# mLSTM queries and keys turned by VectorE's 32x32 squares and transfers through memory, with their copies and convolutions two and three units later

## What is computed

```python
qk, v, o, gates, z = jnp.split(x @ w_in, [o1, o2, o3, o4], axis=-1)   # qk: 8 heads x 128 queries, then keys
qk = jax.nn.silu(_causal_depthwise_conv(qk, conv_w, conv_b))          # 4 taps along the sequence
q, k = jnp.split(qk, 2, axis=-1)
# per head: s_qk = q k^T * exp(gates), then s_qk v, norm, output gates
```

## Time and profile before

| | us |
|---|---|
| median of 3 runs | 1828.47 (1828.24 to 1828.49) |
| the profiled execution, its own time | 1828.43 |
| span of the profiled execution | 1826.6 |
| PE busy | 1813.7 (99% of the span) |
| DVE busy | 1267.3 (69%) |
| ACT busy | 942.7 (52%) |

### The profile page before, as it was taken

How to read it: one execution, slowest core, us unless ns; L and a number is a source line. 1 busy time by engine, 2 the same in 40 slices (tenths; PEclk the granted TensorE clock), 3 DMA queues, 4 the chain that set the end, 5 groups by cost and what they waited for, 6 DMA issues and landing times.

```text
span 1826.6 us, 24598 instructions
## 1 busy us (share of the span) xinstructions
PE 1813.7 (99%) x8999; PEld 1531.1 (84%) x8999; DVE 1267.3 (69%) x1711; ACT 942.7 (52%) x1310; POOL 38.0 (2%) x116
## 2 busy tenths in 40 slices
PE   8999999999999999999999999999999999999999
PEld 7899998888888888887888888888888888888887
DVE  6676766588556755767887878787767556577764
ACT  4545554455465555636554545555435444565542
POOL 2000000000000004000000000000000000000000
PEclk9999999999999999999999999999999999999999
DMA  8565454668889887575555555544547776555453
GB/s 293 162 177 148 139 175 156 202 179 185 177 153 212 175 179 176 191 238 159 174 175 152 167 173 154 179 154 160 185 138 232 217 217 209 162 160 163 159 166 113
DMA packets 172909, 323.61 MB, mean 177 GB/s; under 512 B 16584, under 2 KB 23136, under 8 KB 172048
## 3 DMA queue, kind: packets, MB, share of 16 engines
q1 hardware_dynamic: 171680, 317.89, 60.6%
q10 hardware_dynamic: 576, 4.19, 0.6%
q0 software_dynamic: 560, 0.26, 0.1%
HBM read 318.11 MB, written 4.19 MB: 176 GB/s over the span
## 4 chain that ended last, share of the span: by engine, by line
PE 98%; DVE 1%; ACT 0%; DMA 0%; issue 0%; DVEq 0%
PE acc L366 28%; PE acc L368 28%; PE acc L367 27%; PE ps L615 2%; PE ps L2760 2%; PE ps L463 1%; PE acc L332 1%; PE acc L333 1%; PE acc L331 1%; PE ps L648 1%; PE acc L350 0%; PE acc L349 0%; PE acc L353 0%; PE acc L355 0%; PE acc L348 0%; PE acc L354 0%
## 5 line engine op out<-in xcount | busy, mean ns | idle before, releaser
L299 DVE TENSOR_TENSOR wlo<-wraw,whi 128x1024 fp32r<-128x1024 f32 x579 | 699.1, 1222 | 337.4 <-ACT whi L284 334.4
L284 ACT ACTIVATE whi<-wraw 128x1024 fp32r<-128x1024 f32 x579 | 599.9, 1052 | 365.8 <-PE acc L368 333.4
L366 PE MATMUL acc<-whi,ta_hi 128*128 128x512 f32 x1664 | 659.7, 396 | 3.6 <-DVE ta_lo L548 2.0
L368 PE MATMUL acc<-whi,ta_lo 128*128 128x512 f32 x1664 | 649.2, 390 | 0.0
L367 PE MATMUL acc<-wlo,ta_hi 128*128 128x512 f32 x1664 | 647.8, 389 | 0.0
L366 PEld LDWEIGHTS acc<-whi,ta_hi 128*128 128x128 f32 x1664 | 312.6, 188 | 68.7 <-DVE ta_lo L548 3.4
L368 PEld LDWEIGHTS acc<-whi,ta_lo 128*128 128x128 f32 x1664 | 312.3, 188 | 66.9
L367 PEld LDWEIGHTS acc<-wlo,ta_hi 128*128 128x128 f32 x1664 | 312.8, 188 | 62.1
L366 PE MATMUL acc<-whi,tb_hi 128*128 128x512 f32 x576 | 228.4, 396 | 0.0
L368 PE MATMUL acc<-whi,tb_lo 128*128 128x512 f32 x576 | 224.9, 390 | 0.0
L367 PE MATMUL acc<-wlo,tb_hi 128*128 128x512 f32 x576 | 224.4, 390 | 0.0
(11 more groups left out here) (325 smaller groups left out, 1644.8 us busy)
## 6 DMA issues: line engine op xcount, KB each, us to landing
wraw<-in_ml_w_in SPq DMA_DIRECT2D x129, 512.0 KB, 5.8
wraw<-in_a_w_in SPq DMA_DIRECT2D x128, 512.0 KB, 3.9
wraw<-in_kv_w SPq DMA_DIRECT2D x64, 512.0 KB, 4.0
wraw<-in_b_w_in SPq DMA_DIRECT2D x64, 512.0 KB, 4.4
wraw<-in_mla_w_in SPq DMA_DIRECT2D x49, 512.0 KB, 4.6
wraw<-in_mla_w_out SPq DMA_DIRECT2D x32, 512.0 KB, 3.8
wraw<-in_ml_w_out SPq DMA_DIRECT2D x32, 512.0 KB, 4.4
wraw<-in_a_w_out SPq DMA_DIRECT2D x32, 512.0 KB, 3.8
```

The source lines that it names most:

```text
L284: nc.scalar.activation(unit_of(whi, n, SPLIT, w), unit_of(wraw, n, RAW, w), ACT.Copy).then_inc(w_high, 1)
L299: nc.vector.tensor_tensor(unit_of(wlo, n, SPLIT, w), unit_of(wraw, n, RAW, w), unit_of(whi, n, SPLIT, w).bitcast(F32), ALU.subtract).then_ ...
L366: nc.tensor.matmul(o, xh, wh, start=first, stop=False)
L368: m = nc.tensor.matmul(o, xl, wh, start=False, stop=end)
```

## The change

The eight PE transposes per tile go away, for queries and keys of both halves. In their place DVE turns 32x32 squares of the evacuated tile into `cin` (`qk_square`, two instructions), right after it has copied the tile out of PSUM: DVE's unit 9 and 18 in the first half, 10 and 18 in the second (`QK_EVAC`; for s = 0 it counts places in the phase, 1 and 10). SP writes `cin` to memory after its load 8 places later, and reads it back into `qkw1` with four transfers after its load 10 places later (`turn_qk`). ACT's `window_in` copies from `qkw1` into `cin`, now two instructions of 128x512 from SBUF. `L1_AT` moves: queries from 11 to 13, keys from 19 to 22, and with them `window_in`, `conv`, `conv_sigmoid` and `conv_gate`; `weigh` stays after unit 27.

```diff
-        L1_AT = {"q": 11, "k": 19, "ws": [27, 33, 39, 45], "nm": [31, 37, 43, 49], "g0": 56, "t0": 60}
+        L1_AT = {"q": 13, "k": 22, "ws": [27, 33, 39, 45], "nm": [31, 37, 43, 49], "g0": 56, "t0": 60}
+        QK_EVAC = {(0, 0): 1, (0, 1): 10, (1, 0): 10, (1, 1): 18}
+        def qk_squares_of(v):
+            return cin[:, :, PAD:].rearrange("p j (b h c) -> p b j h c", b=TB, h=4)[:, v]
...
+            def turn_qk(name, p):
+                for (s, j), at in QK_EVAC.items():
+                    n = 2 * s + j
+                    if name == f"l1_{s}" and p == at + 8:
+                        sp.wait_ge(l1["q_sq"], TB * (n + 1))
+                        sp.dma_start(qk_squares.rearrange("p (j r) -> p j r", j=4), cin[:, :, PAD:]).then_inc(l1["q_out"], 16)
+                    if name == f"l1_{s}" and p == at + 10:
+                        sp.wait_ge(l1["q_out"], 16 * (n + 1))
+                        for i in range(4):
+                            rows = qkw1[32 * i:32 * i + 32, 1024 * j:1024 * j + 1024]
+                            sp.dma_start(rows.rearrange("q (i r) -> q i r", i=4),
+                                         qk_squares.rearrange("(i q) (j r) -> j q i r", i=4, j=4)[i]).then_inc(l1["q_in"], 16)
...
             def window_in(s, j):
                 n = 2 * s + j
-                act.wait_ge(l1["q_pe"], n + 1)
-                if n > 0:
-                    act.wait_ge(l1["y_ok"], 4 * n)
+                act.wait_ge(l1["q_in"], 64 * (n + 1))
                 act.wait_ge(l1["pads"], 2)
-                nc.scalar.activation(cin[:, :, PAD:], ps2(0).rearrange("p (h t) -> p h t", t=T),
-                                     ACT.Copy).then_inc(l1["q_c"], 1)
+                y = qkw1[:, 1024 * j:1024 * j + 1024].rearrange("p (i b h c) -> p b h i c", i=4, b=TB, h=4)
+                for b in range(TB):
+                    nc.scalar.activation(cin[:, :, PAD + b * P:PAD + (b + 1) * P].rearrange("p h (i c) -> p h i c", i=4),
+                                         y[:, b], ACT.Copy).then_inc(l1["q_c"], 1)
...
+            def qk_square(s, j):
+                landed(dve, *l1_at(s, j))
+                if 2 * s + j > 0:
+                    dve.wait_ge(l1["y_ok"], 4 * (2 * s + j))
+                for b in range(TB):
+                    v = qkw[j][:, b, :].rearrange("p (h j c) -> p j h c", h=4, j=4)
+                    nc.vector.transpose(qk_squares_of(b), v).then_inc(l1["q_sq"], 1)
...
-            def window(s, j):
-                landed(pe, *l1_at(s, j))
-                pe.wait_ge(tr_lo, turn.n)
-                if 2 * s + j > 0:
-                    pe.wait_ge(l1["q_c"], 2 * s + j)
-                if s > 0:
-                    pe.wait_ge(l1["st"], 4 * s)
-                for h in range(4):
-                    for b in range(TB):
-                        m = nc.tensor.transpose(ps2(0)[:, h * T + b * P:h * T + (b + 1) * P],
-                                                qkw[j][:, b, h * P:(h + 1) * P], ident[:])
-                m.then_inc(l1["q_pe"], 1)
...
             def weigh(s, c):
                 h = c % 4
                 pe.wait_ge(l1["q_r"], 2 * s + 2)
-                pe.wait_ge(l1["q_c"], 2 * s + 2)
+                if h == 0:
+                    pe.wait_ge(tr_lo, turn.n)
...
-                for j in range(2):
-                    if u == L1_AT["qk"[j]]:
-                        window(s, j)
```

More of the change, by code:

```diff
@@ L112, in build @@
         ARENA = 14016
+        qk_squares = nc.dram_tensor("qk_squares", (P, 2 * COLS), F32).ap()
         arena = sb("arena", [P, ARENA])
@@ L794, in build @@
         L1_GATES = ("l1_g", 1)
-        l1 = sems(1, "g_in g_pe g_row g_e g_m g_pe2 g_col q_pe q_c y_ok y_e q_r sc arg ex sel st nm "
+        QK_EVAC = {(0, 0): 1, (0, 1): 10, (1, 0): 10, (1, 1): 18}
+        def qk_squares_of(v):
+            return cin[:, :, PAD:].rearrange("p j (b h c) -> p b j h c", b=TB, h=4)[:, v]
+        l1 = sems(1, "g_in g_pe g_row g_e g_m g_pe2 g_col q_sq q_out q_in q_c y_ok y_e q_r sc arg ex sel st nm "
                      "den h ssq var rs og ge z_ok pads")
@@ L1051, in _ @@
                         load(name, p)
+                        turn_qk(name, p)
                 else:
@@ L2011, in gates_c @@
                 nc.vector.tensor_copy(acol, ps[:, 3, 0:16].rearrange("p (b h) -> p b h", b=TB)).then_inc(l1["g_col"], 1)
+            def qk_square(s, j):
[5 more added lines that the diff above has]
+                    nc.vector.transpose(qk_squares_of(b), v).then_inc(l1["q_sq"], 1)
             def conv(s, j, heads):
                 n = 2 * s + j
-                dve.wait_ge(l1["q_c"], n + 1)
+                dve.wait_ge(l1["q_c"], TB * (n + 1))
                 if s > 0:
@@ L2096, in l1_side @@
                 u = p if s else p + 8
+                for j in range(2):
+                    if p == QK_EVAC[(s, j)]:
+                        qk_square(s, j)
                 if s == 0 and p == 4:
```

## The result

| | before | after |
|---|---|---|
| median, us | 1828.43 (6 runs, 1828.24 to 1828.57) | 1836.34 (6 runs, 1833.83 to 1839.70) |
| ratio | 1 | 1.0044, 95% interval 1.0034 to 1.0054 |
| profiled execution, us (span) | 1828.43 (1826.6) | 1833.83 (1832.1) |

The kernel became slower by 0.44%, 8 us, and its time, which before repeated within 0.3 us, spreads over 6. The forecast was 1829.5, no change. The profiled execution is the fastest of the six, 2.5 us under the median: the delays in its trace are smaller than those of a median run.

What follows compares the result with a forecast made beforehand. PE, busy 99% of the span, was taken to bound the kernel. Windows -3.5, waits at `weigh` +2.0 and +1.3, late reads +1.2 sum to +1.0 us: median 1828.47 becomes 1829.5, range 1826.6 to 1832.6.

Steps and rivals of the forecast that it cites:

- what the four windows cost PE: PE's transposes of queries and keys in both halves: removing four windows at 0.87 us each gives -3.5 us.
- the rival that each transpose costs its length: PE's transposes cost their full 272 ns each, -8.7 us in place of -3.5, time 1824.3; chance 0.02.
- the squares at nothing: DVE's squares take 1.2 us a tile in a stream where DVE idles, so they add no time.
- the fixed price of moving the convolutions three units while `weigh` stays: PE waits at first-head `weigh` for the moved keys' chain: 2.0 us in the first half, 1.3 in the second.
- the gain goes into two waits at `weigh`: The author's main forecast: the windows' gain becomes new PE waits at both `weigh`s, time 1827 to 1832; chance 0.68.
- +1.2 us: Second half's keys: last read lands about 1.2 us after ACT wants it, adding in full to PE's wait at `weigh`.
- rival B: Second half's keys' reads land 4 us or more late behind slow loads: +4.3, 1832.8 us; chance 0.20.
- for the queries the reads are issued some 5 units ahead and I find them landed, or less than 1 us late: Queries' reads before ACT's copy: any lateness under 1 us, beneath 2.1 us of cover on PE.
- -11.1: Time in us, relative to PE's start on unit 22 (Z), when SP issues the second half's keys' write.
- 7.9 (from -5.5 to +2.4): Second half's keys: us from first read issue to last landing, counted from PE's start on unit 22.
- ACT and DVE have split up to 3 units ahead, so nothing else becomes late: Behind the waiting `weigh`: splits run far enough ahead that no other PE work waits; none of the wait is won back.

Runs made afterwards that it cites:

- experiment 5: Changed kernel without the write and reads back (ACT copies unturned data), queries and keys at the old places 11 and 19: 1825.25 us, ratio 0.9982.
- experiment 2: Changed kernel without the write to memory and the reads back; ACT copies unturned data, convolutions stay at the moved places: 1829.06 us, ratio 1.0006.
- Experiment 3: Kernel before with only the schedule numbers moved (queries 11 to 13, keys 19 to 22), PE still transposing: 1835.40 us, ratio 1.0038.
- Experiment 6: Changed kernel with the four reads issued after SP's load 9 places behind the squares instead of 10: 1828.96 us, ratio 1.0007.
- experiment 1: The changed kernel run again with no edit, for a second profile and the spread: 1835.02 us, ratio 1.0042.
- experiment 4: Changed kernel with the first head's `weigh` of each half after PE's unit 28 instead of 27: 1831.25 us, ratio 1.0016.
- experiment 10: Repeat of the changed kernel with reads 9 places behind the squares instead of 10: 1829.23 us, 11 runs in two groups.
- experiment 9: Changed kernel with reads 9 places behind the squares, plus 12 unused PE transposes ahead of each first-head `weigh`: 1828.81 us, ratio 1.0002.
- experiment 8: Changed kernel with the four reads issued by POOL in its own queue once the write has landed, instead of by SP: 1840.68 us, ratio 1.0064.
- Experiment 7: Changed kernel with reads 9 places behind the squares instead of 10 and the first head's `weigh` one unit later: 1825.15 us, ratio 0.9982.

## Why the prediction was wrong

**Right, to 0.3 us:** what the four windows cost PE (-3.5 forecast, -3.2 in experiment 5; the rival that each transpose costs its length is out), the squares at nothing (experiment 5), and the fixed price of moving the convolutions three units while `weigh` stays (2.0 and 1.3 forecast, 1.89 and 1.31 in experiment 2). Experiment 3 shows that price without squares and transfers (waits of 2.27 and 2.47, against 2.2 and 2.7 expected). The mechanism was the forecast's too: the gain goes into two waits at `weigh`, and the late reads add to the second one.

**Wrong: the term "+1.2 us" for the reads of the second half's keys.** They were 4.26 and 4.44 us late, which is past the 3.9 from which rival B was to decide. The step failed in two places. First, "for the queries the reads are issued some 5 units ahead and I find them landed, or less than 1 us late". They were issued 6.25 us, 2.3 units, ahead (591.12, where ACT was ready at 599.02 - 1.65 = 597.37), and were 1.65 late; experiments 1 and 4 show 2.17 and 2.54. The cover on PE took most of it, and some 0.15 us came through at unit 19. But the convolution, the squares and the write of the keys stand behind them on DVE and SP, so the keys' write was issued at Z - 9.4 and not at -11.1. A lateness that PE is nearly covered against was handed on to a step that has no cover. Second, with two loads between write and reads the reads took 10.0 us from the first issue (616.43) to ACT's start (626.44), where I had 7.9 (from -5.5 to +2.4). The write itself landed in 5.0 us, 0.6 less than I had counted. So 1.7 - 0.6 + 2.1 = 3.2, which is the difference between 4.3 and 1.2 to within 0.1. Experiment 6 shows both steps by removing them: the write goes 2.0 us sooner, the reads land 2.5 us faster, and the wait is gone.

**Wrong: "ACT and DVE have split up to 3 units ahead, so nothing else becomes late".** With 1.2 us of lateness it would have held, by an estimate: 3.1 us less of lateness against waits of 0.40 and 2.09. With 4.3 the splits of units 26 and 27 came after PE. It changed where PE waited and not how long: the sum at `weigh` is still 1.3 + 4.3.

**Missing: the clock.** Waits of 1.9 us and more at PE were followed in some executions by a stretch at the lower clock. In the changed kernel's profile it lies behind the 2.09 us wait for unit 27:

```profile
638.23 0.40 PE L367 MATMUL acc<-whi,ta_hi 128*128 128x512 f32 x1
638.47 0.59 PE L368 MATMUL acc<-wlo,ta_hi 128*128 128x512 f32 x1
638.86 0.63 PE L369 MATMUL acc<-whi,ta_lo 128*128 128x512 f32 x1
```

Starts go from 0.23 to 0.43 us apart for eight products: 8 x 0.2 = 1.6 us. In this execution it cost nothing, since `weigh` had still 0.87 us to wait; so the fastest run is explained by the waits alone. In the upper group's run of experiment 10 it comes behind the first `weigh`, where nothing hides it. That it makes the two groups 1.5 us apart is shown by experiments 9 and 10 and by the clocks that all runs list.

**The spread of 6 us** goes with the late reads. The changed kernel and experiments 1 and 4, whose reads come late, spread over 3.7 to 5.9 us (experiment 8 over 1.8 in four runs). Without transfers, or with the reads in time, the times lie within 0.6 us or in groups some 1.5 us apart (experiments 2, 3, 5, 6, 7, 9, 10). And the 1.15 us between the two profiled runs are the reads' lateness (experiment 1). How late the reads are in the slowest runs, what part the clock has there, and why the lateness varies from run to run, no trace shows.

The Trainium skill's rule that descriptors on a DMA engine are consumed in ring order (page "DMA: Bandwidth & Descriptors", Queues, rings and completion order) agrees with experiment 6, where one load fewer ahead made the reads 2.4 to 2.9 us faster. It is a rule on one ring. What I concluded from it, that reads in another queue get past the loads, did not hold in experiment 8: 10.1 us.

**Where the expected gain went,** in the fastest run (1833.83, 5.4 us above the kernel before): 3.2 us won at the windows; 3.8 lost to the place of `weigh`, slow starts included (experiment 2 against 5); 4.3 to the late reads of the second half's keys and some 0.5 to the other late reads. The median run is another 2.5 us slower, in shares of lateness and clock that are open. Experiment 7 keeps the gain by removing both losses.

## What to carry to other kernels

When a step is moved later, measure the spare time of its last consumer (5.3 us here) against the move (8.2 us), and move the consumer too if it has room: here `weigh` could go one unit later at no cost. For a round trip through memory, count the transfers in flight when the reads are issued and put the reads ahead of the next prefetch; one load fewer ahead of each turn's reads was worth 6 us in all, and another queue made it worse. Follow a lateness that looks covered to the next link of its chain.

## What I had not expected of the hardware

A wait of 1.9 to 2.5 us on PE, in a stream otherwise full, is followed in some executions by some 3 us at 1.2 GHz (granted clock 0.51 to 0.63, products 0.43 us apart) and in others of the same kernel by none (experiments 2, 6, 10: 3 of 11, 5 of 11, 5 of 11 runs in the slower group). Where nothing hides it, the price is 1.5 us a time. Not every such wait had it: 2.10 and 2.55 us in the first half of the changed kernel's two profiles did not. Twelve useless transposes in the wait removed it.

Reads issued on POOL's queue landed in 10.1 us, against 6.5 on SP's behind two loads and 4.0 behind one. Issuing a read on SP took 0.35 to 0.43 us each with one load ahead, and up to 1.29 us with two (the second half's keys).
